# Gathering an expert's tokens in fp32 from the residual rows, with the reciprocal root inside the one-hot, in place of three bf16 pieces

## The reference, cut to what matters

```python
hn = rmsnorm(h, norm_ffn_g[l])                 # (h * rsqrt(mean(h*h) + eps)) * g
h = h + moe_ffn(hn, w_router[l], b_router[l], w_gate_up[l], b_gate_up[l], w_down[l], b_down[l])
# moe_ffn: logits = hn @ w_router + b_router; top 4 of 32; softmax over the four
#   for each expert:  hgu = hn @ wgu + bgu            wgu: 1024 x 2048
#                     y = ((up + 1) * (gate * sigmoid(1.702 * gate))) @ wd + bd     wd: 1024 x 1024
#                     acc += gates[:, expert] * y
```

## Time and profile before

| | |
|---|---|
| median of 3 runs | 1175.51 us (1175.22 to 1176.18) |
| the profiled execution: its own time | 1172.28 us |
| the profiled execution: its span | 1170.7 us |
| busy over the span | PE 92%, PEld 41%, DVE 17%, ACT 13%, POOL 2% |
| DMA | 437.18 MB, 373 GB/s on the mean |

### The profile page before, as it was taken

One profiled execution on the slowest core, in us unless ns is written; L12 is line 12 of the kernel. 1 busy time (PEld: TensorE's weight loads), 2 busy tenths in 40 slices (PEclk: granted clock), 3 DMA queues, 4 the chain that ended last, 5 costly groups with the idle time before them and its releaser, 6 DMA issues.

```text
span 1170.7 us, 15024 instructions
## 1 busy us (share of the span) xinstructions
PE 1079.7 (92%) x6238; PEld 483.7 (41%) x6238; DVE 204.2 (17%) x434; ACT 152.9 (13%) x327; POOL 27.8 (2%) x71
## 2 busy tenths in 40 slices
PE   8999999989999988888888888888888888888896
PEld 6677888543333333333333333333333333333332
DVE  2312213123111111111111111111111111111112
ACT  1244221230000000000000000000000000000002
POOL 0010000210000000000000000000000000000000
PEclk9999999989999999999999999999999999999999
DMA  9961527379999999999999999999999999999992
GB/s 321 333 259 72 216 96 275 141 322 420 427 428 428 429 429 428 427 429 429 429 429 428 428 428 430 428 429 429 428 427 430 429 429 429 428 427 429 387 427 100
DMA packets 44457, 437.18 MB, mean 373 GB/s; under 512 B 5337, under 2 KB 6417, under 8 KB 19633
## 3 DMA queue, kind: packets, MB, share of 16 engines
q1 hardware_dynamic: 42256, 435.19, 89.1%
q10 hardware_dynamic: 2176, 1.65, 0.6%
HBM read 435.76 MB, written 1.06 MB: 373 GB/s over the span
## 4 chain that ended last, share of the span: by engine, by line
DMA 55%; PE 43%; DVE 1%; ACT 0%; issue 0%; SPq 0%; POOL 0%; DVEq 0%; POOLq 0%
DMA ring<-in_w_down_dram 54%; PE bank L1299 12%; PE bank L1055 9%; PE bank L1271 9%; PE bank L1153 2%; PE bank L1165 2%; PE bank L1058 2%; PE bank L1251 1%; PE bank L1242 1%; DMA ring<-in_w_in_dram 1%; PE bank L1290 0%; PE bank L1123 0%; PE bank L1098 0%; PE bank L1263 0%; PE bank L1353 0%
## 5 line engine op out<-in xcount | busy, mean ns | idle before, releaser
L1271 PE MATMUL bank<-ring,gates 128*64 128x512 f32 x2048 | 466.8, 598 | 0.0
L1299 PE MATMUL bank<-ring,gates 128*64 128x512 f32 x1024 | 232.0, 597 | 72.3 <-DMA ring<-in_w_down_dram 72.3
L1271 PEld LDWEIGHTS bank<-ring,gates 128*64 128x64 f32 x2048 | 139.3, 137 | 238.3 <-issue 227.7
L1299 PEld LDWEIGHTS bank<-ring,gates 128*64 128x64 f32 x1024 | 69.0, 136 | 233.6 <-issue 117.2
L927 DVE TENSOR_SCALAR gates<-bank 128x512 f32<-128x512 f32 x32 | 22.1, 692 | 756.3 <-PE bank L1271 756.3
L1055 PE MATMUL bank<-ring 128*128 128x256 f32 x384 | 85.0, 381 | 0.0
L1055 PEld LDWEIGHTS bank<-ring 128*128 128x128 f32 x384 | 72.3, 190 | 11.3 <-issue 1.3
L1251 PE MATMUL bank<-gates,scatter_w 64*128 64x512 f32 x256 | 63.6, 615 | 0.7 <-ACT gates L675 0.7
L671 ACT ACTIVATE gates<-gates 128x512 f32<-128x512 f32 x32 | 20.1, 630 | 275.4 <-DVE gates L927 275.4
L1242 PEld LDWEIGHTS bank<-onehot,qkT 128*128 128x128 bf16 x1488 | 45.1, 98 | 25.1 <-issue 25.1
L675 ACT ACTIVATE gates<-bank 128x512 f32<-128x512 f32 x32 | 19.1, 597 | 260.7 <-PE bank L1299 260.7
(11 more groups left out here) (181 smaller groups left out, 518.4 us busy)
## 6 DMA issues: line engine op xcount, KB each, us to landing
ring<-in_w_gate_up_dram SPq DMA_DIRECT2D x128, 2048.0 KB, 26.0
ring<-in_w_down_dram SPq DMA_DIRECT2D x63, 2048.0 KB, 25.5
ring<-in_w_in_dram SPq DMA_DIRECT2D x9, 2048.0 KB, 21.9
ring<-in_w_out_dram SPq DMA_DIRECT2D x1, 4096.0 KB, 12.7
ring<-in_w_in_dram SPq DMA_DIRECT2D x4, 512.0 KB, 7.5
ring<-in_w_proj_sb_dram SPq DMA_DIRECT2D x1, 2048.0 KB, 10.0
ring<-in_w_proj_moba_dram SPq DMA_DIRECT2D x1, 2048.0 KB, 7.5
ring<-in_w_down_dram SPq DMA_DIRECT2D x2, 1024.0 KB, 20.1
```

Of the source, the lines that this page charges most:

```text
L1271: ins = mm(bank[4 + i][SLOTS * c:SLOTS * (c + 1), :], xeT[:, k, :], ring[:, base + k // 2, n0:n0 + CH], start=False, stop=k == KD - 1)
L1299: ins = mm(bank[6][SLOTS * c:SLOTS * (c + 1), :], rows, ring[:, place, j * D + c * CH:j * D + (c + 1) * CH], start=k == 0, stop=k == KD - 1)
```

## The change

The three pieces are gone, and with them all that made them and waited for them on the scalar engine, GpSimd and the vector engine. The gather reads the fp32 rows `resid` themselves, which hold h without the reciprocal root; the one-hot becomes fp32 and holds the token's reciprocal root where it held 1. So a gather is 8 x 2 = 16 fp32 products with weights of 128 x 128 and 64 streamed columns. `one_hots` is two instructions (one for each group of tokens) that compare and multiply, where it was one that compared. `first_gather` is gone; expert 0 uses `gather`. The load of the down bias (128 KB, issued by the scalar engine) moves ahead to stand behind the second part of the squares, since the place that it writes is no longer used by the pieces.

```diff
-        onehot = sb("onehot", [P, NT, SLOTS], BF16)
+        onehot = sb("onehot", [P, NT, SLOTS])
...
@@ gpsimd
-            pool.wait_ge(rstd_rd, 1)
-            scaled_rows(0, slice(0, D))
-            left_over(0, 0, slice(0, D), 1)
-            left_over(1, 0, slice(0, D), 2)
-            pool.wait_ge(rstd_rd, 2)
-            scaled_rows(1, slice(CH, D))
-            left_over(0, 1, slice(CH, D), 5)
-            left_over(1, 1, slice(CH, D), 7)
...
@@ scalar
             square_part(1)
+            act.dma_start(bdown_sb, b_down[0]).then_inc(late_in, 16)
             root(0)
-            first_piece(0, slice(0, D))
             turned(1)
             square_part(2)
-            next_piece(1, 0, slice(0, D), left_p, 1)
             turned(2)
-            next_piece(2, 0, slice(0, D), left_p, 2)
-            act.wait_ge(piece_rd, 3)
-            act.dma_start(bdown_sb, b_down[0]).then_inc(late_in, 16)
             square_part(3)
             turned(3)
             root(1)
-            first_piece(1, low)
-            first_piece(1, high)
-            next_piece(1, 1, low, left_d, 1)
-            next_piece(1, 1, high, left_p, 3)
-            next_piece(2, 1, low, left_d, 2)
-            next_piece(2, 1, high, left_p, 4)
             act.wait_ge(routed, NT)
...
@@ vector
             choose(1)
-            dve.wait_ge(piece_rd, 4)
-            V.scalar_tensor_tensor(out=res2[1][:, 0:CH], in0=resid[:, 1, 0:CH], scalar=stat[:, 33:34],
-                                   in1=pieces[0][:, 1, 0:CH], op0=ALU.mult, op1=ALU.subtract).then_inc(left_d, 1)
             dve.wait_ge(consts2, 3)
...
-                return V.tensor_tensor(onehot[:, :, :], slot_no[:, :, 0:SLOTS],
-                                       rank[:, :, bass.ds(col, 1)].to_broadcast([P, NT, SLOTS]), ALU.is_equal)
+                for t in range(NT):
+                    ins = V.scalar_tensor_tensor(out=onehot[:, t, :], in0=slot_no[:, t, 0:SLOTS],
+                                                 scalar=rank[:, t, bass.ds(col, 1)],
+                                                 in1=stat[:, 32 + t:33 + t].to_broadcast([P, SLOTS]),
+                                                 op0=ALU.is_equal, op1=ALU.mult)
+                return ins
...
                 one_hots(0).then_inc(onehot_rd, 1)
-                if r is None:
-                    dve.wait_ge(piece_rd, 6)
-                    V.tensor_tensor(res2[1][:, 0:CH], res2[1][:, 0:CH], pieces[1][:, 1, 0:CH], ALU.subtract
-                                    ).then_inc(left_d, 1)
...
@@ tensor
             def gather(count):
 
                 pe.wait_ge(onehot_rd, count)
                 for k in range(KD):
-                    for i in range(3):
-                        for t in range(NT):
-                            n = i * NT + t
-                            ins = mm(bank[7][:, k * SLOTS:(k + 1) * SLOTS], pieces[i][:, t, 2 * P * (k // 2) + k % 2:2 * P * (k // 2 + 1):2],
-                                     onehot[:, t, :], start=n == 0, stop=n == 3 * NT - 1)
+                    c0 = 2 * P * (k // 2) + k % 2
+                    for t in range(NT):
+                        ins = mm(bank[7][:, k * SLOTS:(k + 1) * SLOTS], resid[:, t, c0:c0 + 2 * P - 1:2], onehot[:, t, :],
+                                 start=t == 0, stop=t == NT - 1)
                 ins.then_inc(gathered, 1)
...
-                if r is None:
-                    first_gather()
-                else:
-                    gather(done + 1)
+                gather(done + 1)
```

More of the change, by code:

```diff
@@ L155, in hybrid_layer @@
         gslot = sb("gslot", [P, KD // 2, 2])
-        pieces = [qkT[:, 4 * i:4 * i + 4, :].bitcast(BF16).rearrange("p a b -> p (a b)")
-                  .rearrange("p (t d) -> p t d", t=NT) for i in range(3)]
         gatesT = gates[:, :, :].rearrange("p t d -> p (t d)").rearrange("p (g n) -> p g n", n=T)
@@ L171, in hybrid_layer @@
         bdown_sb = qkT[0:E, 12:16, :].rearrange("p a b -> p (a b)")
-        res2 = [qkT[:, 12:16, :].rearrange("p a b -> p (a b)"), gates[:, 0, 0:D]]
         trash = [t.rearrange("p t n -> p (t n)").bitcast(BF16) for t in
@@ L248, in hybrid_layer @@
         count_rd = sem("count_rd")
-        piece_rd = sem("piece_rd")
         bgu_rd = sem("bgu_rd")
@@ L255, in hybrid_layer @@
         rstd_rd = sem("rstd_rd")
-        left_p = sem("left_p")
-        left_d = sem("left_d")
         onehot_rd = sem("onehot_rd")
@@ L618, in root @@
                                      ).then_inc(rms_std, 1)
[L620 to L629, removed]
             square_part(0)
@@ L1218, in _ @@
             ins.then_inc(rank_ps, 1)
-            def first_gather():
-                pe.wait_ge(onehot_rd, 1)
-                for t in range(NT):
-                    for i in range(3):
-                        for k in range(KD):
-                            if t == 0 and i == 0 and k == 0:
-                                pe.wait_ge(piece_rd, 3)
-                            if t == 1 and k % 4 == 0:
-                                pe.wait_ge(piece_rd, 4 + 2 * i + k // 4)
-                            ins = mm(bank[7][:, k * SLOTS:(k + 1) * SLOTS], pieces[i][:, t, 2 * P * (k // 2) + k % 2:2 * P * (k // 2 + 1):2],
-                                     onehot[:, t, :], start=t == i == k == 0, stop=t == NT - 1 and i == 2,
-                                     skip_group_check=True)
-                ins.then_inc(gathered, 1)
             def gather(count):
```

## The result

The changed kernel takes 1185.68 us (median of 4 runs, 1185.11 to 1186.05) against 1175.37 for the kernel before beside it: ratio 1.0085, with a 95% interval of 1.0069 to 1.0100. It is slower, as forecast, but by 10 us (0.0085 of 1175) and not by 4. The profiled execution has a span of 1184.2 us where that of before had 1170.7. Of the 13.5, 0.7 us stand ahead of the change already (the router's last products start at 235.81, not 235.08).

A forecast was written before the change was run, and what follows sets the result against it. The prediction took the stream of weights to bound the kernel, only in the middle. Transition -0.3, start of the stream +2.3 and tail +2.1 gave +4.1 us, thus 1179.6 us, with a range of 1176.5 to 1183.2.

The forecast's parts named there:

- the transition: About 236 to 250 us, before the weight stream starts: first gather ends and `take` starts 0.3 us sooner, -0.3.
- the +1.8 case: First gather at half clock: weight loads take 0.224 us, gather 7.2, `take` 3.3 later, about 1.5 given back: +1.8.
- the clock at the transition is better than I take it: Rival: full clock from the first gather on, total +2.4 us, 1177.9; chance 0.08.
- its signs of being wrong: Gather under 2.5 or over 4.3 us, low clock stretch much shorter or longer than 10 us, or one in the passes.
- The start of the stream, 2.3 us: First loads behind the transition: longer gathers delay the stream by 2.3 us, bounds 1.3 and 3.3.
- The gather, 3.6 us,: Each new fp32 gather: 32 instructions at 0.112 us, 3.6 us in all, 2.1 more than now.
- The tail, 2.1,: Behind the last wait for a load: one gather on the tensor engine's chain, +2.1 us.
- the tensor engine's start 1.0 us sooner: At the transition: the tensor engine starts the first gather at about 238.5 in place of 239.51, 1.0 us sooner.
- the first wait for down weights gone: Steady passes: longer gather hidden, first wait (1.73 us) gone, second about 1.2, price 0.
- the moved load: Down bias load, 128 KB, issued earlier on the scalar queue: price 0.
- the tensor engine becomes the bound: Rival, steady passes: a gather above 4.3 us exceeds the spare time; at 0.17 us an instruction +38, 1214; chance 0.07.
- The anchor: Whole kernel: the runs' median lies 3.2 us above the profiled time, and the same distance was added to the forecast.

The follow-up runs named there:

- mid_bf16: Changed kernel with the gathers for experts 5 to 30 made of 48 bf16 products, precision left out: 1186.03 us, ratio to the kernel before 1.0100.
- after: The changed kernel itself, with fp32 gathers and no further edit: 1185.68 us, ratio to the kernel before 1.0085.
- after_fill: Changed kernel plus ten fp32 filler products of constants where the tensor engine waits at the transition: 1180.82 us, ratio to the kernel before 1.0053.
- after_fill_rows: Changed kernel plus the ten fillers, with the down bias's products over all 128 array rows in place of 32: 1178.42 us, ratio to the kernel before 1.0028.
- before_fill_rows: Kernel before plus fifteen fillers at the transition, with the down bias's products over 128 array rows: 1172.78 us, ratio to the kernel before 0.9974.
- early_fill_rows: after_fill_rows with the gathers for experts 1, 2 and 3 made of 48 bf16 products: 1174.93 us, ratio to the kernel before 1.0001.
- mid_more: Changed kernel with the gathers for experts 5 to 30 made of 24 fp32 products in place of 16: 1218.29 us, ratio to the kernel before 1.0364.
- last_fill_rows: after_fill_rows with the gather for expert 31 alone made of 48 bf16 products: 1175.68 us, ratio to the kernel before 1.0008.
- after_bias: Changed kernel with the down bias and its vector engine sums moved from the end of gate_up(0) to that of gate_up(1): 1187.36 us, ratio 1.0114.

## Why the prediction was wrong in size

The forecast was +4.1 us, and the measurement is 10.0 by the ratio. The direction and the places were right: the loss is the price of the fp32 gather in front of the first eight loads and behind the last one, and 26 gathers between cost nothing (mid_bf16). The mechanism was right at the full clock and wrong at half clock.

**The step that failed is the transition, "I take -0.3 and keep +1.8 for the range".** It took the weight load to be as long at half clock as at the full one. It is 0.222 us against 0.125 (after and after_fill). The upper bound named that case and sized the load well (0.224), but it let 1.5 us come back when the clock rises at 246.90, as in the trace of before, and came to +1.8. In the changed kernel the clock rose at 252.3, and `gate_up(0)` up to the gather took 10.63 us in place of 9.84: between the two profiled executions the term was 3.1 + 0.8 = +3.9. The low stretch was held fixed while the work under it changed.

The prediction says that no row at half clock shows the weight load. The trace of the kernel before had some, two fp32 loads each of 128x64 in `gate_up(0)`, ahead of the rise and behind it:

```profile
245.15 0.26 PEld L1271 LDWEIGHTS bank<-ring,gates 128*64 128x64 f32 x2 [0.59 <-issue]
...
247.76 0.15 PEld L1271 LDWEIGHTS bank<-ring,gates 128*64 128x64 f32 x2 [0.27 <-issue]
```

They take 0.26 us at half clock and 0.15 at the full one, which speaks for the +1.8 case. By the Trainium skill's formula for the weight load (TensorE: Matmul & The Clock Gate, LDWEIGHTS), 128 columns take one fixed time; the trace disagrees at half clock, where 32 loads took 7.11 us, and the measurement decides. At the full clock the term was right within the uncertainty: 2 us more for the first gather, 1.2 to 2.6 less for the pieces. By the traces, from the router's last products to `take` it is 7.5 us both in after_fill_rows and in before_fill_rows.

**The second low stretch was not in the sum at all.** It costs 1.7 us in the profiled execution (5.13 less 3.44). The kernel before seems to have it in some executions too, so it isn't all a price of the change: the profiled execution had none, but 29 of the 87 others on record have a granted clock of 0.991 or less where the profiled one has 0.993. The rival "the clock at the transition is better than I take it" had a chance of its own, and a clock that stays low for longer had none, though the prediction names it among its signs of being wrong. The two profiled executions would put 3.9 + 0.3 and 1.7 us on the clock, 5.9 over the forecast; the runs bear out some 4. All that hangs on the clock is 10.0 - 6.3, some 4 us: after_fill_rows gives back 0.0057, 6.7 us, of which the kernel before would get 3.1 too.

**The start of the stream, 2.3 us, was probably too small, by 0.5 to 1:** it is 3.2 to 3.5 by early_fill_rows, with 1.8 us of uncertainty, and 2.8 by the shift of the last wait for a load between before_fill_rows and after_fill_rows. The slack in front of the load of 282.55 was taken as 2.3 us, from the difference of two landings (10.1 and 7.8); in the changed kernel that load still took 9.4 where an unqueued one took 7.7. I read this as slack that was never there, but no run tests it. The term stayed within its bounds of 1.3 and 3.3, near the upper one.

**The gather, 3.6 us,** is 3.91: 0.122 us for an instruction, not 0.112. The loads of the new gather, and those of the fillers in after_fill:

```profile
712.95 3.85 PEld L1179 LDWEIGHTS bank<-onehot,resid 128*128 128x128 f32 x32 [0.81 <-issue]
...
236.66 1.20 PEld L1164 LDWEIGHTS bank<-neg_tri,neg_one 128*128 128x128 f32 x10
```

With 0.20 and 0.19 us for the last load they follow each other by 0.118 and 0.112. The fillers stream 128 columns and the router 32, both from packed weights, and both have 0.112, so the number of streamed columns doesn't explain the 0.118. The step of two words in the weights may: L1290, with a step of four, has 0.117 by the prediction's own working. The rest up to 0.122 is the start and the drain. **The tail, 2.1,** is 2.4 because the gather is longer.

Right: the tensor engine's start 1.0 us sooner (0.9: the gather at 239.31 less 0.7 of shift ahead of it, against 239.51); the first wait for down weights gone, the second smaller than said (0.79, not 1.2); the period of the stream unchanged; the moved load free; no low stretch from 300 us to the last microseconds. The rival "the tensor engine becomes the bound" is borne out as a mechanism: it put the threshold at a gather of 4.3 us, 3.91 costs nothing in the middle, and mid_more, with 5.87, came to 1218.3 where the spare time of the changed kernel's passes gave 1220. The threshold itself was not tested.

The anchor was off too: the prediction carried the distance of 3.2 us between one profiled execution and the median over as a constant. It is mostly the spread of the kernel's own low stretches: the 29 executions of the kernel before with a granted clock of 0.991 or less took 1176.8 us on the mean, the 58 others 1174.2. The changed kernel's profiled execution (1185.94) stands at its median.

Open: why the low stretches begin and end where they do. early_fill_rows and last_fill_rows have one of 3.4 us near 244 us in spite of the fillers, before_fill_rows still spreads over 5 us, and the distance of 20.5 us between the end of one stretch and the start of the next, in five of the nine traces, is not explained.

## What to carry to other kernels

In a kernel bound by its stream of weights, an operation costs time where it stands in front of the first loads that depend on compute, and behind the last one. In between it is free until the pass exceeds the stream's period, and from there it costs in full. Not every microsecond in front of the first loads counts, as after_bias shows. Price an operation at the clock that its place will have, and ask what the edit does to that clock: near a short wait of the tensor engine, take both levels as cases with chances of their own. A product that moves may have been covering someone else's wait.

## What the runs showed of the hardware

An instruction of an fp32 product, with a weight load of 128 x 128 and 64 streamed columns, took 0.122 to 0.125 us at 2.4 GHz and 0.222 at 1.2 GHz; a bf16 product of this shape took 0.031 to 0.038 at 2.4 GHz. 48 bf16 products whose weights are read with a step of four elements and whose one-hots with a step of two took 1.69 to 1.80 us at 2.4 GHz and 2.3 to 2.4 at 1.2 GHz; with a step of two and a packed one-hot they took 1.51 at 2.4 GHz.

Half-clock stretches came behind products that use 32 rows of the array as well as behind waits: they were there in nine of eleven traces, and none was at that place in the five kernels in which the same products ran over 128 rows. One came at the new place when the products were moved, but one stayed at the old place too. Besides the mean clocks of whole executions, one trace for each kernel is all that this rests on, so the rows of the array are a likely cause and not a shown one.
